# Two layers of a hybrid decoder on one core: the routing's combining weights made and spread behind the first two expert products

## The chip, the cores and the metric

The kernel runs on one core of a Trainium2 chip, as one program written by hand for five engines: TensorE (PE in the profile), VectorE (DVE), ScalarE (ACT), GpSimd (POOL) and SyncE (SP), which issues the large transfers. The metric is the device time of one execution in microseconds (us), lower is better.

## The reference

Two layers (`DEPTH = 2`) over 256 prompt tokens and 32 sample tokens, model width 1024, all in float32. Each layer mixes the tokens with three kinds of recurrent heads, projects back, normalises, and then sends each token through two of 32 experts. The expert part is what the change touches:

```python
def _moe(h, router_w, router_bias, p):
    scores = jax.nn.sigmoid((ht @ router_w).astype(jnp.float32))
    choice = (scores + router_bias.astype(jnp.float32)).reshape(T, N_EXPERT_GROUPS, EXPERTS_PER_GROUP)
    ...
    expert_idx = g_idx * EXPERTS_PER_GROUP + local
    wts = jnp.take_along_axis(scores, expert_idx, axis=1)
    wts = wts / jnp.sum(wts, -1, keepdims=True)
    ...
    def expert_block(args):
        xb, e = args
        return (jax.nn.silu(xb @ p["e_gate"][e]) * (xb @ p["e_up"][e])) @ p["e_down"][e]
    ...
    contrib = (ys[dest] * wts.reshape(A)[order][:, None]).astype(ht.dtype)
```

Of an expert, gate and up are 1024 x 512 and down is 512 x 1024: 2 MB each, 6 MB an expert, 32 experts a layer.

## The kernel before

There is no scheduler. Each engine's program is a function (`_(sp)`, `_(pe)`, `_(act)`, `_(dve)`, `_(pool)`), its instructions run in the order in which the code stands, and engines wait for each other by semaphores. `Signal.at(l, k)` is the k-th event of layer `l`; `stand(eng)` marks a wait in a way that has no part in the result. Of PSUM's eight banks six rotate through a list, `bank_plan()`: each entry names a result and who takes it away ("A" ScalarE, "D" VectorE). `emptied(l, key)` is the event that the bank which `key` will fill is free, `takes(l, key)` that `key` has been taken away, `fills(l, key)` that TensorE has filled it.

At the end of a layer's mixer the routing runs like this. TensorE turns the normalised rows (`turn_half`, `turn_few`, result `h2t`), multiplies them with the router (`logits`: 24 products for three tiles of tokens, tile 0 and 1 with 128 tokens, tile 2 with 32), turns the rows back (`turn_back`, `back`) and spreads the gate rows (`spread`). VectorE picks two experts a token from the scores (`oh_ready` when it is done). TensorE then counts with triangular products which place each token has in its expert's block (`rank`), and VectorE makes of it the 0/1 matrix `sel` (`select`), with which TensorE gathers the tokens of 4 experts into slots (`gather`, 32 slots an expert, `BLK`; a quad of experts is 128 slots). ScalarE copies the gathered rows in two halves into `xTb` (`take_gather`; events `g_half` and `g_taken`). Beside that, VectorE makes the two combining weights of each token (`dtm[:, 1]`), lays them on diagonals (`diagonal(1)`, event `wdiag_ready`), and TensorE spreads them over all partitions with a product with ones (`rows_of`, results `wrow` 0 and 1, which VectorE copies into `dbc`). The same is done for slot numbers (`diagonal(0)`, `ddiag_ready`, `drow_full`). From `dbc` VectorE builds `selw`, which spreads the experts' outputs back to the tokens (`weights`, `spread_out`). VectorE also scales the normalised rows (`x1_done`) and plans the blocks that overflow (`bew`, `bei`, `npi`, event `plan_ready`).

The experts then go in pairs `d`, member `b`, with two weight buffers, `ring` for `b` = 0 and `ring1` (printed `ring_122`) for `b` = 1, each with room for gate, up and down of one expert. `gate_up` waits for the weights (`gu_full`), multiplies, and signals `u_full`; ScalarE's `silu` and VectorE's `hidden` follow; `down` multiplies with the down weights (`dn_full`) and signals `d_full`. SP orders gate and up of the next expert for a buffer at `u_full`, its down at `d_full`. The down weights of expert 2 alone have a place of their own, `early`, and are ordered once, ahead of the loop. `keep_clock(n)` is filler on TensorE: n products of 512 columns whose result nobody reads. In the first quad of experts SP's order is:

```python
                sp.wait_ge(x1_done.sem, x1_done.at(l, 1))
                idle["sp"].stand(sp)
                sp.dma_start(early[:].rearrange("p (k n) -> p k n", n=D_MODEL),
                             A["exp_w_down"][l, 2].rearrange("(p k) n -> p k n", k=4)).then_inc(early_full.sem, 16)
                sp.wait_ge(u_full, 2 * (seen + 1) + 1)
                experts(0, 2)
                sp.wait_ge(u_full, 2 * (seen + 1) + 2)
                experts(1, 3)
                sp.wait_ge(d_full, 2 * (seen + 1) + 2)
                experts_down(1, 3)
```

## Time and profile before

| | before |
|---|---|
| median of 3 runs | 1876.62 us (1869.5 to 1877.93) |
| profiled execution, own time | 1879.24 us |
| its span | 1877.4 us |
| granted TensorE clock, mean | 0.9 of full |
| PE busy | 1545.1 us, 82% |
| DVE busy | 744.8 us, 40% |
| ACT busy | 346.8 us, 18% |
| DMA, mean over the span | 302 GB/s, 567.56 MB |

The profile is of one execution, on the hardware. Busy shares are means over stages that have different limits: TensorE's 82% doesn't say that it is the limit of any one of them. A float32 product appears as two instructions in the trace, so that the 24 router products are 48 rows' worth; the order of the built program, shown below, counts each once.

### The profile page before, as it was taken

To read this page: it belongs to the slowest core of one execution; us is meant where nothing else is said; L and a number is where in the kernel's file an instruction comes from. 1 tells how busy PE (TensorE), PEld (TensorE's weight loads), DVE (VectorE), ACT (ScalarE), POOL (GpSimd) and SP (SyncE) were. 2 spreads that over 40 slices of the span, in tenths; PEclk is the share of its full clock that TensorE was granted. 3 is DMA by queue.
4 is the path that set the end of the run, shared out by engine and by line. 5 is a ranking of instruction groups with operands and counts; after the bars stand their busy time and mean duration, and the time that the engine had idled before them with its cause. 6 is when DMAs were issued, how large, how long until landed. Compare 5 with 4: busy or idle time off the path is not lost.

```text
span 1877.4 us, 29665 instructions
## 1 busy us (share of the span) xinstructions
PE 1545.1 (82%) x11834; PEld 849.0 (45%) x11834; DVE 744.8 (40%) x1706; ACT 346.8 (18%) x787; POOL 116.8 (6%) x168
## 2 busy tenths in 40 slices
PE   5999999998867776677889999999976677666795
PEld 2764543545433333334366555354543334333442
DVE  0253565767312221222535266585732222122226
ACT  0235321203101111010223532120210111011001
POOL 4000002200200000000020000211000000000000
PEclk8899999988978888888989899998988889888877
DMA  9453447557999999999954543746789999999993
GB/s 321 152 191 139 124 127 209 167 198 293 380 405 427 428 428 428 428 429 428 401 210 164 200 124 101 224 127 227 285 347 427 428 428 428 428 427 428 429 426 129
DMA packets 94567, 567.56 MB, mean 302 GB/s; under 512 B 8245, under 2 KB 9021, under 8 KB 69138
## 3 DMA queue, kind: packets, MB, share of 16 engines
q1 hardware_dynamic: 82578, 532.05, 70.2%
q0 software_dynamic: 11904, 34.34, 6.5%
q8 instruction: 57, 0.93, 0.2%
q14 instruction: 28, 0.23, 0.0%
HBM read 550.55 MB, written 15.81 MB: 302 GB/s over the span
## 4 chain that ended last, share of the span: by engine, by line
PE 52%; DMA 38%; DVE 5%; issue 2%; SPq 1%; DVEq 1%; ACT 1%; ACTq 0%
DMA ring<-in_exp_w_up 35%; PE ps L1550 10%; PE ps L1017 9%; PE ps L992 9%; PE ps L1387 3%; PE ps L1239 3%; DMA ring<-in_w_ada 3%; PE ps L856 2%; PE ps L999 2%; PE ps L1208 1%; PE ps L1143 1%; PE ps L1184 1%; PE ps L1373 1%; PE ps L1567 1%; SPq L623 1%
## 5 line engine op out<-in xcount | busy, mean ns | idle before, releaser
L1550 PE MATMUL ps<-ring,xTb 128*32 128x256 f32 x4224 | 332.2, 484 | 232.8 <-DMA ring<-in_exp_w_up 220.6
L1550 PEld LDWEIGHTS ps<-ring,xTb 128*32 128x32 f32 x4224 | 164.7, 138 | 400.2 <-issue 357.8
L2745 DVE TENSOR_TENSOR hb<-sg,ps 128x128 f32<-128x128 f32 x66 | 25.0, 379 | 475.4 <-ACT sg L1932 475.4
L1017 PE MATMUL ps<-ring,hT 128*128 128x512 f32 x384 | 171.4, 599 | 0.0
L992 PE MATMUL ps<-hT,ring 128*128 128x288 f32 x640 | 165.0, 417 | 4.7 <-DVE hT L2089 2.5
L1523 PE MATMUL ps<-sel,h_tm 128*128 128x128 f32 (+1 forms) x912 | 162.9, 306 | 0.0
L1523 PEld LDWEIGHTS ps<-sel,h_tm 128*128 128x128 f32 x912 | 124.4, 188 | 52.8 <-issue 22.6
L992 PEld LDWEIGHTS ps<-hT,ring 128*128 128x128 f32 x640 | 122.7, 194 | 42.6 <-issue 8.4
L1932 ACT ACTIVATE sg<-ps 128x128 f32<-128x128 f32 x66 | 18.3, 277 | 605.1 <-PE ps L1550 605.1
L1567 PE MATMUL ps<-ring,hTb 128*32 128x256 f32 x2048 | 126.7, 389 | 2.5 <-DVEq L2748 2.5
L2753 DVE COPY ys<-ps 32x256 f32<-32x256 f32 x124 | 52.6, 424 | 161.1 <-PE ps L1567 159.9
L1017 PEld LDWEIGHTS ps<-ring,hT 128*128 128x128 f32 x384 | 71.1, 190 | 98.7 <-issue 98.2
L1675 ACT ACTIVATE ys<-ps 32x256 f32<-32x256 f32 x140 | 52.2, 373 | 217.9 <-PE ps L1567 216.6
L1582 PE MATMUL ps<-ys,selw 128*128 128x512 f32 x136 | 69.5, 639 | 20.6 <-DVEq L2754 20.5
L1567 PEld LDWEIGHTS ps<-ring,hTb 128*32 128x32 f32 x2048 | 60.8, 111 | 46.2 <-issue 3.7
L856 PE MATMUL ps<-ring,cT 128*32 128x512 f32 x384 | 54.5, 674 | 14.9 <-DMA ring<-in_w_ada 14.6
L1239 PE MATMUL ps<-ring,hT 128*128 128x512 f32 x128 | 62.3, 644 | 2.8 <-DVE h_tm L2310 2.8
L2771 DVE TENSOR_TENSOR acc<-acc,ps 128x512 f32<-128x512 f32 x68 | 46.8, 688 | 39.8 <-PE ps L1582 39.8
L2126 DVE SCALAR_TENSOR_TENSOR cv<-raw,vecT,cv 128x312 f32<-128x312 f32 x96 | 52.2, 543 | 7.2
L1582 PEld LDWEIGHTS ps<-ys,selw 128*128 128x128 f32 x136 | 22.4, 194 | 62.2 <-issue 38.1
L1239 PEld LDWEIGHTS ps<-ring,hT 128*128 128x128 f32 x128 | 25.9, 208 | 33.7 <-issue 30.2
L2292 DVE TENSOR_TENSOR h0s<-h0s,tbh 128x512 f32<-128x512 f32 x32 | 22.2, 692 | 42.8 <-PE ps L1184 40.1
(503 smaller groups left out, 1687.7 us busy)
## 6 DMA issues: line engine op xcount, KB each, us to landing
ring<-in_exp_w_gate SPq DMA_DIRECT2D x66, 2048.0 KB, 18.7
ring<-in_exp_w_up SPq DMA_DIRECT2D x66, 2048.0 KB, 23.2
ring<-in_exp_w_down SPq DMA_DIRECT2D x64, 2048.0 KB, 24.8
ring<-in_w_ada SPq DMA_DIRECT2D x24, 2048.0 KB, 10.2
ring<-in_w_in SPq DMA_DIRECT2D x22, 2048.0 KB, 9.1
ring<-in_w_out SPq DMA_DIRECT2D x8, 2048.0 KB, 9.1
h0s<-in_state_ssd POOLq DMA_DIRECT2D x16, 512.0 KB, 7.2
out_ssd_s<-h0s POOLq DMA_DIRECT2D x16, 512.0 KB, 5.3
```

Source lines behind the costliest of these rows:

```text
L856: mm(o[32 * g:32 * g + 32, :], cT[:, k, :], w[:, k, :], start=(r == 0), stop=False, skip_group_check=True)
L992: last = mm(o[:, 0:T], w[:, k, m * P:(m + 1) * P], hT[:, k, :], start=(k == 0), stop=(k == KT - 1))
L1017: last = mm(o[:, :], hT[:, k, T0[i]:T0[i] + P], w[:, k, :], start=(k == 0), stop=(k == KT - 1))
L1239: last = mm(o[:, :], hT[:, k, T0[i]:T0[i] + P], w[k // 4][:, k % 4, a * 512:(a + 1) * 512], start=(k == 0), stop=(k == KT - 1))
L1387: last = mm(o[:, :], y(k, i), w[k // 4][:, k % 4, a * 512:(a + 1) * 512], start=(k == 0), stop=(k == 7))
L1523: last = mm(o, h_tm[0:ROWS[i], i, k * P:(k + 1) * P], sel[0:ROWS[i], i, 0:n], start=(i == 0), stop=(i == NT - 1))
L1550: last = mm(ps[32 * j:32 * j + 32, b, 0:2 * P], xTb[:, k, m * BLK:(m + 1) * BLK], w[:, 0:2, k * D_EXPERT + j * P:k * D_EXPERT + (j + 1) * ...
L1567: last = mm(ps[32 * c:32 * c + 32, 2 + b, 0:2 * P], hTb[:, b, j * BLK:(j + 1) * BLK], w[:, j * D_MODEL + c * 256:j * D_MODEL + (c + 1) * 256],
L1582: last = mm(o[:, :], selw[:, T0[i]:T0[i] + P], ys[:, a * 512:(a + 1) * 512], start=True, stop=True)
L1675: cp = lambda o_, i_: f(o_, i_, ACT.Copy)
L2126: stt(c_, r_[:, j:j + CVW], tap(j), c_, ALU.mult, ALU.add)
L2753: cpy(ys[m * BLK:(m + 1) * BLK, c * 256:(c + 1) * 256], ps[32 * c:32 * c + 32, 2 + b, 0:2 * P])
```

## The change

It moves work about within the routing and the first quad, in both layers, and adds or drops almost nothing:

- Four of tile 0's eight router products go ahead of the second tile's transposes, behind `keep_clock`, which there goes from 3 to 1 products.
- On VectorE the combining weights and their diagonals move from ahead of the rank to behind the scaling of the rows. The copy of the counts (`nblk`) moves from behind that scaling to ahead of it, and the plan of overflowing blocks (`block_plan`) into the first quad.
- On TensorE the weights' rows are no longer spread ahead of the gather, in `wrow` banks, but behind the first two gate and up products, together with the slots' rows, in banks 3, 4 and 5. Bank 3 is also the second down product's, which gets a wait for `drow_taken`.
- The first gate and up product waits for the first half of the gathered rows, and in its middle for the second.
- The order of the first quad becomes: product 0, product 1, rows, down 0, down 1, gather of half the next quad, product 2, two of the gather, down 2, product 3, two of the gather, down 3. ScalarE and VectorE follow it.
- `early` is loaded in two halves; the first no longer waits for `x1_done`.

The diff, cut to its core (the `stand` marks and the old waits for the `wrow` banks are left out):

```diff
-    out += [(("rank",), "D"), (("wrow", 0), "D"), (("wrow", 1), "D")]
+    out += [(("rank",), "D")]
...
                 sp.wait_ge(filled.sem, fills(l, ("back", 1, 1)))
                 idle["sp"].stand(sp)
+                third = early[:].rearrange("p (k n) -> p k n", n=D_MODEL)
+                third_src = A["exp_w_down"][l, 2].rearrange("(p k) n -> p k n", k=4)
+                sp.dma_start(third[:, 0:2, :], third_src[:, 0:2, :]).then_inc(early_full.sem, 16)
                 sp.wait_ge(x1_done.sem, x1_done.at(l, 1))
                 idle["sp"].stand(sp)
-                sp.dma_start(early[:].rearrange("p (k n) -> p k n", n=D_MODEL),
-                             A["exp_w_down"][l, 2].rearrange("(p k) n -> p k n", k=4)).then_inc(early_full.sem, 16)
+                sp.dma_start(third[:, 2:4, :], third_src[:, 2:4, :]).then_inc(early_full.sem, 16)
...
                 turn_few()
-                keep_clock(3)
+                pe.wait_ge(*emptied(l, ("logit",)))
+                pe.wait_ge(*takes(l, ("h2t", 0, 0)))
+                logits(0, range(4))
+                keep_clock(1)
...
-                keep_clock(2)
-                pe.wait_ge(wdiag_ready.sem, wdiag_ready.at(l, 1))
-                rows_of(bank(("wrow", 0)), 2, 0)
-                rows_of(bank(("wrow", 0)), 2, 1).then_inc(FL, 1)
-                rows_of(bank(("wrow", 1)), 2, 2).then_inc(FL, 1)
-                keep_clock(2)
+                keep_clock(4)
...
-                pe.wait_ge(*takes(l, ("wrow", 1)))
+                pe.wait_ge(*takes(l, ("ms", 10)))
+                pe.wait_ge(*takes(l, ("rank",)))
...
                     for k in range(KT):
+                        if k == KT // 2 and second_half is not None:
+                            pe.wait_ge(g_taken, second_half)
...
+                def first_quad():
+                    d0, d1 = pe.snap(pairs + 0), pe.snap(pairs + 1)
+                    pe.wait_ge(g_half.sem, g_half.at(l, 1))
+                    gate_up(d0, 0, 0, steady + 1)
+                    gate_up(d0, 1, 1)
+                    pe.wait_ge(wdiag_ready.sem, wdiag_ready.at(l, 1))
+                    rows_of(ps[:, 3, :], 2, 0)
+                    rows_of(ps[:, 3, :], 2, 1)
+                    rows_of(ps[:, 5, 2 * TS:], 2, 2)
+                    pe.wait_ge(ddiag_ready.sem, ddiag_ready.at(l, 1))
+                    rows_of(ps[:, 4, :], 0, 0)
+                    rows_of(ps[:, 4, :], 0, 1)
+                    rows_of(ps[:, 5, :], 0, 2).then_inc(drow_full.sem, 1)
+                    down(d0, 0)
+                    pe.wait_ge(drow_taken.sem, drow_taken.at(l, 1))
+                    down(d0, 1)
+                    pe.wait_ge(sel_ready, steady + 2)
+                    gather(0, 4, QS).then_inc(gq_full.sem, 1)
+                    gate_up(d1, 0, 2)
+                    gather(4, 6, QS)
+                    down(d1, 0, True)
...
                 for k in range(2):
-                    tt(rt[:, 5 + k], rt[:, 3 + k], rt[:, 0], ALU.mult)
-                D()
-                for k in range(2):
-                    V.tensor_reduce(dtm[:, 1, :, k], rt[:, 5 + k], AX_X, ALU.add)
-                D()
...
-                diagonal(1)
-                D().then_inc(wdiag_ready.sem, 1)
...
                 select(QS, 0)
+                cpy(nblk[:, 0, :], bank(("rank",))[:, 96:128]).then_inc(TD, 1)
...
                 dve.sem_inc(x1_done.sem, 1)
...
+                diagonal(1)
+                D().then_inc(wdiag_ready.sem, 1)
```

Three places in the built program's order. The first is TensorE between the first transposes of the turned rows (`ps<-con,x_tm`) and the end of the router products (`ps<-rw,hT`); `ps<-con` alone is filler. Before:

```order
L1430 MATMUL ps<-con,x_tm 128x128 x8
L1438 MATMUL ps<-con,x_tm 128x32 x8
L914 MATMUL ps<-con 128x512 x3
L1430 MATMUL ps<-con,x_tm 128x128 x8
L1444 MATMUL ps<-rw,hT 128x32 x8
L1444 MATMUL ps<-rw,hT 32x32 x8
L1444 MATMUL ps<-rw,hT 128x32 x8
```

and of the changed kernel:

```order
L1432 MATMUL ps<-con,x_tm 128x128 x8
L1440 MATMUL ps<-con,x_tm 128x32 x8
L1446 MATMUL ps<-rw,hT 128x32 x4
L916 MATMUL ps<-con 128x512
L1432 MATMUL ps<-con,x_tm 128x128 x8
L1446 MATMUL ps<-rw,hT 128x32 x4
L1446 MATMUL ps<-rw,hT 32x32 x8
L1446 MATMUL ps<-rw,hT 128x32 x8
```

Four router products have moved ahead, and two filler products are gone.

The second is TensorE from the last rank product to the second down product: `ps<-diag,con` and `ps<-diag_s,con` are the rows of weights or slots, `ps<-sel,h_tm` the gather, `ps<-ring,xTb` gate and up, `ps<-ring,hTb` down. Before:

```order
L1496 MATMUL ps<-rt,con 128x32
L914 MATMUL ps<-con 128x512 x2
L1502 MATMUL ps<-diag,con 128x256 x2
L1504 MATMUL ps<-diag_s,con 128x64
L914 MATMUL ps<-con 128x512 x2
L1536 REGISTER_ALU
L1523 MATMUL ps<-sel,h_tm 128x128 x24
L1546 ISA
L1547 ISA
L1550 MATMUL ps<-ring,xTb 32x256 x32
L1502 MATMUL ps<-diag,con 128x256 x2
L1504 MATMUL ps<-diag_s,con 128x64
```

which goes on with 6 gather products, the first down product and the second gate and up product. Of the changed kernel, from the filler on:

```order
L916 MATMUL ps<-con 128x512 x4
L1532 REGISTER_ALU
L1519 MATMUL ps<-sel,h_tm 128x128 x24
L1544 ISA
L1545 ISA
L1551 MATMUL ps<-ring,xTb 32x256 x32
L1545 REGISTER_ALU
L1551 MATMUL ps<-ring_122,xTb 32x256 x32
L1507 MATMUL ps<-diag,con 128x256 x2
L1509 MATMUL ps<-diag_s,con 128x64
L1507 MATMUL ps<-diag,con 128x256 x2
L1509 MATMUL ps<-diag_s,con 128x64
```

Both sets of rows stand behind two gate and up products, and the filler is in one piece.

The third is VectorE from the choice of experts (`rt<-rt 128x32`) to the first reading of the ranks (`rt<-rt,ps`). Before:

```order
L2613 TENSOR_TENSOR rt<-rt 128x32
L2621 TENSOR_TENSOR rt<-rt 128x96 x2
L2624 TENSOR_REDUCE dtm<-rt 128x3 x2
L2626 TENSOR_TENSOR stat<-dtm 128x3
L2628 TENSOR_TENSOR rt<-rt,nblk 128x96 x2
L2630 RECIPROCAL stat<-stat 128x3
L2632 TENSOR_REDUCE stat<-rt 128x3 x2
L2634 TENSOR_TENSOR dtm<-dtm,stat 128x6
L2642 TENSOR_TENSOR diag<-con,dtm 128x128 x4
L2642 TENSOR_TENSOR diag_s<-con,dtm 32x32 x2
L2651 TENSOR_TENSOR rt<-rt,ps 128x64
```

and of the changed kernel:

```order
L2645 TENSOR_TENSOR rt<-rt 128x32
L2653 TENSOR_TENSOR rt<-rt,nblk 128x96 x2
L2656 TENSOR_REDUCE stat<-rt 128x3 x2
L2670 TENSOR_TENSOR rt<-rt,ps 128x64
L2671 TENSOR_TENSOR rt<-rt,ps 32x32
L2670 TENSOR_TENSOR rt<-rt,ps 128x64
```

The weights and their diagonals are gone from here; they now follow the four multiplications that scale the rows.

## Rows read from the trace of the kernel before

**Rows 1.** The page: GB/s in 40 equal slices of the span.

```profile
GB/s 321 152 191 139 124 127 209 167 198 293 380 405 427 428 428 428 428 429 428 401 210 164 200 124 101 224 127 227 285 347 427 428 428 428 428 427 428 429 426 129
```

**Rows 2.** The page: the chain that ended last, by engine and line.

```profile
DMA ring<-in_exp_w_up 35%; PE ps L1550 10%; PE ps L1017 9%; PE ps L992 9%; PE ps L1387 3%; PE ps L1239 3%; DMA ring<-in_w_ada 3%; PE ps L856 2%; PE ps L999 2%; PE ps L1208 1%; PE ps L1143 1%; PE ps L1184 1%; PE ps L1373 1%; PE ps L1567 1%; SPq L623 1%
```

**Rows 3.** Windows around the routing of layer 0.

```profile
core 0: us, PE busy (x) PEld busy (x) DVE busy (x) ACT busy (x) POOL busy (x), PEclk, DMA share, GB/s
437.50:440.50 3.00, 3.00 (x16) 2.77 (x16) 1.03 (x4) 1.26 (x4) 0.00 (x0) 0.50 1.03 437
445.00:454.00 9.00, 9.00 (x37) 5.16 (x37) 7.88 (x34) 1.17 (x2) 0.00 (x0) 1.00 1.00 427
455.00:458.00 3.00, 3.00 (x19) 2.40 (x18) 2.63 (x6) 0.60 (x1) 0.00 (x0) 1.00 0.04 16
458.50:463.50 5.00, 2.25 (x14) 1.63 (x12) 4.28 (x19) 1.88 (x2) 0.00 (x0) 0.78 0.84 347
464.50:473.00 8.50, 7.47 (x68) 3.69 (x68) 2.62 (x7) 0.28 (x1) 0.00 (x0) 0.58 0.01 3
474.00:500.00 26.00, 22.54 (x325) 13.73 (x325) 8.03 (x19) 3.01 (x10) 4.42 (x9) 1.00 0.99 419
```

**Rows 4.** Timeline of SP, layer 0: start and length in us.

```profile
457.20 0.33 SPq L649 DMA_DIRECT2D early<-in_exp_w_down  x1
472.21 0.33 SPq L623 DMA_DIRECT2D ring<-in_exp_w_gate  x1
...
481.05 0.33 SPq L623 DMA_DIRECT2D ring<-in_exp_w_gate  x1
...
490.13 0.34 SPq L623 DMA_DIRECT2D ring<-in_exp_w_gate  x1
```

**Rows 5.** Timeline of PE, layer 0; idle time before and its releaser in brackets.

```profile
433.57 4.76 PE L1444 MATMUL ps<-rw,hT 128*128 128x32 f32 x48
...
447.07 1.98 PE L914 MATMUL ps<-con 128*128 128x512 f32 x4
448.92 1.10 PE L1502 MATMUL ps<-diag,con 128*128 128x256 f32 x4
...
450.31 1.98 PE L914 MATMUL ps<-con 128*128 128x512 f32 x4
452.24 8.51 PE L1523 MATMUL ps<-sel,h_tm 128*128 128x128 f32 x48
465.53 6.61 PE L1550 MATMUL ps<-ring,xTb 128*32 128x256 f32 x64 [4.78 <-DVE dbc L2734]
472.07 1.13 PE L1502 MATMUL ps<-diag,con 128*128 128x256 f32 x4
473.13 0.43 PE L1504 MATMUL ps<-diag_s,con 32*128 32x64 f32 x2
473.49 2.18 PE L1523 MATMUL ps<-sel,h_tm 128*128 128x128 f32 x12
475.60 1.93 PE L1567 MATMUL ps<-ring,hTb 128*32 128x256 f32 x32
477.35 3.64 PE L1550 MATMUL ps<-ring,xTb 128*32 128x256 f32 x64
```

**Rows 6.** Timeline of PE, layer 1.

```profile
1353.06 8.41 PE L1523 MATMUL ps<-sel,h_tm 128*128 128x128 f32 x48
1366.08 5.20 PE L1550 MATMUL ps<-ring,xTb 128*32 128x256 f32 x64 [4.61 <-DVE dbc L2734]
```

**Rows 7.** Timeline of SP, layer 1.

```profile
1371.35 0.33 SPq L623 DMA_DIRECT2D ring<-in_exp_w_gate  x1
```

**Rows 8.** Timeline of DVE, layer 0: first look at the ranks, last step of `sel`.

```profile
448.72 0.22 DVE L2651 TENSOR_TENSOR rt<-rt,ps 128x64 f32<-128x64 f32 x1
...
451.60 0.56 DVE L2675 TENSOR_TENSOR sel<-selt 128x384 f32<-128x384 f32 x1
```

**Rows 9.** Timeline of ACT, layer 0: gate rows and second gathered half.

```profile
445.01 1.19 ACT L1916 ACTIVATE gate<-ps 32x512 f32<-32x512 f32 x2 [0.40 <-PE ps L881]
...
460.79 0.60 ACT L1675 ACTIVATE xTb<-ps 128x512 f32<-128x512 f32 x1 [3.62 <-PE ps L1523]
```

More of the change, by code:

```diff
@@ L1465, in _ @@
                     turn_half(1, a)
-                pe.wait_ge(*emptied(l, ("logit",)))
-                idle["pe"].stand(pe)
                 pe.wait_ge(*takes(l, ("h2t", 0, 1)))
                 idle["pe"].stand(pe)
-                logits(0, range(KT))
+                logits(0, range(4, KT))
                 pe.wait_ge(*takes(l, ("h2t", 2)))
@@ L1938, in take_down, with quad @@
                     last.then_inc(ysa, 1)
-                with act.Fori(0, QUADS) as Q:
+                def quad(Q, first):
                     d0 = act.snap(pairs + 2 * Q)
+                    if first:
+                        for b in range(2):
+                            silu(d0, b)
                     for m in range(QUAD):
                         d, b = d0 + m // 2, m % 2
-                        silu(d, b)
+                        if not first or m > 1:
+                            silu(d, b)
                         if m == QUAD - 1:
@@ L2685, in _ @@
                 dve.sem_inc(x1_done.sem, 1)
-                cpy(nblk[:, 0, :], bank(("rank",))[:, 96:128]).then_inc(TD, 1)
-                D()
+                for k in range(2):
+                    tt(rt[:, 5 + k], rt[:, 3 + k], rt[:, 0], ALU.mult)
+                D()
+                for k in range(2):
+                    V.tensor_reduce(dtm[:, 1, :, k], rt[:, 5 + k], AX_X, ALU.add)
+                D()
+                tt(n1, dtm[:, 1, :, 0], dtm[:, 1, :, 1], ALU.add)
+                D()
+                V.reciprocal(n2, n1)
+                D()
+                tt(dtm[:, 1], dtm[:, 1], over(n2, 2), ALU.mult)
+                D()
+                diagonal(1)
+                D().then_inc(wdiag_ready.sem, 1)
                 ts(npi[:], nblk[:, 0, :], float(BLK - 1), None, ALU.add)
@@ L2738, in _ @@
                 spreads = dve.snap(tb + l * QUADS)
-                dve.wait_ge(gq_full.sem, gq_full.at(l, 2))
-                idle["dve"].stand(dve)
                 def hidden(d, b):
@@ L2774, in add_up, with first_quad, quad @@
                         D().then_inc(acc_taken, 1)
-                def quad(Q, first):
+                def first_quad():
+                    d0, d1 = dve.snap(pairs + 0), dve.snap(pairs + 1)
+                    for b in range(2):
+                        hidden(d0, b)
+                    dve.wait_ge(drow_full.sem, drow_full.at(l, 1))
+                    idle["dve"].stand(dve)
+                    for v, at in ((2, 3), (0, 4)):
+                        for i in range(2):
+                            cpy(dbc[:, v:v + 2, T0[i]:T0[i] + P], ps[:, at, i * 2 * P:(i + 1) * 2 * P].rearrange(
+                                "p (v t) -> p v t", v=2))
+                    cpy(dbc[:, 0:2, T0[2]:T], one_rows(ps[:, 5, 0:2 * TS]))
+                    cpy(dbc[:, 2:4, T0[2]:T], one_rows(ps[:, 5, 2 * TS:4 * TS]))
+                    D().then_inc(drow_taken.sem, 1)
+                    dve.wait_ge(gq_full.sem, gq_full.at(l, 2))
+                    idle["dve"].stand(dve)
+                    select(QS, QS)
+                    for b in range(2):
+                        take_down(d0, b, b)
+                    block_plan()
+                    V.memset(acc[:], 0.0)
+                    V.memset(accs[:], 0.0)
+                    weights(QS)
+                    for b in range(2):
+                        hidden(d1, b)
+                        take_down(d1, b, 2 + b)
+                        if b == 0:
+                            dve.sem_inc(early_used.sem, 1)
+                    add_up(spreads)
+                def quad(Q):
                     d0 = dve.snap(pairs + 2 * Q)
@@ L2782, in quad @@
                         if m == 0:
[L2783 to L2792 removed]
                             weights(QS)
                         take_down(d, b, m)
[L2795 to L2796 removed]
                     add_up(spreads + Q)
[L2799 removed]
+                first_quad()
                 with dve.Fori(1, QUADS) as Q:
[L2801 removed]
+                    quad(Q)
                 tail = dve.value_load(npi[0:1, 0:1], min_val=2, max_val=TAILMAX)
```

98 lines of the change are left out of this document (39 added, 59 removed).

## The prediction, made before the changed kernel ran

> **What bounds the kernel now.** I read the page first. Its row of GB/s [rows 1] has two long stretches at 427 to 429 and, before each, a valley with slices down to 100 to 230. The flat stretches are the expert products, whose weights stream in; the valleys are the mixers. The chain that ended last [rows 2] gives 35% of the span to one transfer, `ring<-in_exp_w_up`, far ahead of any line of TensorE. So in the flat stretches the stream of weights is the clock of the kernel: an instruction that ends earlier there is worth nothing unless the stream then starts earlier or pauses less. The question for this change is therefore when the stream stands still near the routing, and whose signal restarts it.
>
> The windows answer it [rows 3]: in layer 0 the stream runs at 427 GB/s from 445 to 454, carries 16 GB/s from 455 to 458, runs again in 458.5 to 463.5 (one piece of 2 MB, `early`), and from 464.5 to 473 carries 3 GB/s. From 474 on it is full again at 419. So about 14 us of layer 0 pass with idle DMA engines, in two pauses. The issues on SP [rows 4] give their ends: `early` goes out at 457.20, and the next weights (expert 2) at 472.21, when the first gate and up product is done. Between that issue and 490.13 nothing is late, since each order falls while the one before still flows.
>
> What makes 472.21 is read on TensorE [rows 5]: the gather starts at 452.24 and runs 8.51 us; then TensorE stands idle 4.78 us, and the row names the releaser, VectorE's copy of the spread weights into `dbc` (the `wrow` banks, which VectorE empties only after its whole block plan); then the first product takes 6.61 us, although the same 64 instructions take 3.64 us at 477.35. The difference is the granted clock, 0.58 in the window 464.5 to 473 [rows 3], half speed for most of it, after the idle time. Layer 1 is the same picture [rows 6]: gather at 1353.06, 4.61 us idle, product 5.20 us, order at 1371.35 [rows 7].
>
> **The change, part by part, as the time of the order for expert 2.**
>
> 1. Upstream of the gather, logits. Four of the 24 logit products (8 of 48 instructions) move ahead of the second transposes, where filler stood, and two of three filler products go. The 48 take 4.76 us [rows 5], so 8 are 0.8 us. The remaining logits need the same transposes as before, so the last logit comes 0.8 us earlier, and what follows in order on TensorE (turning back, spreading, the rank products) with it. The ranks end, read as the start of the filler at 447.07, near 446.3.
>
> 2. Between ranks and gather. Before: filler 1.98, weight rows from 448.92, filler again from 450.31, gather at 452.24 [rows 5], 5.2 us. After: four filler products in one go, twice 1.98 = 3.96, so TensorE is free at 450.3. VectorE's side: from its first look at the ranks at 448.72 to the end of `sel` (451.60 + 0.56) it needs 3.4 us [rows 8], and it no longer makes the combining weights and their diagonals before that look, so it looks when the ranks are there, near 446.5, and is done near 450.0. The gather starts at 450.3: 1.9 us earlier (0.8 of it from point 1).
>
> 3. Gather to first product. The wait on `dbc` is gone: minus 4.78 and 4.61 us [rows 5, 6]. What is asked instead is the first half of the gathered rows, copied by ScalarE while the second half is still gathered, and, in the middle of the product, the second half. That second copy starts at 460.79 and takes 0.60 us [rows 9]; the gather ended at 460.75, so the half is there about 0.65 us after the gather, and TensorE asks for it after half a product, 1.8 us. No wait; if the product did have to wait for it whole, 0.65 us would come back. I take off 4.6 a layer, leaving 0.1 for the signals.
>
> 4. The first product at full clock. With no idle time ahead of it, it should take the 3.64 us of the row at 477.35: minus 3.0 in layer 0, minus 1.6 in layer 1 (5.20). The bound below is nothing, if the clock falls anyhow.
>
> Sum: 1.9 + 4.7 + 3.0 = 9.6 us in layer 0, 1.9 + 4.5 + 1.6 = 8.0 in layer 1, together 17.6 us. The order for expert 2 falls at about 462.6 instead of 472.21.
>
> 5. The early piece in two halves. Its first half no longer waits for the normalised rows and queues behind the weights that flow until some 454.5 [rows 3]; the second goes out when the rows are scaled, 2 us earlier than 457.20 (the selection is 1.9 us earlier, its four multiplications are unmoved). 2 MB at 427 is 4.9 us, so both are in by about 460, ahead of the new order at 462.6. They fill a pause and cost and bring nothing; had the piece been left whole, the result would be the same to a microsecond. If they collide it is for at most 1 us a layer.
>
> 6. What the moved work costs behind the first products. The weights' chain and diagonals (from `rt` to `diag`, some 3 us) now stand behind the scaling on VectorE, ahead of the slot diagonals, whose end stays near 462. TensorE does two products first (until 466), then both sets of rows, 1.13 + 0.43 each [rows 5], until 469, the down product 1.93, a wait of a few tenths for VectorE's six copies out of the bank which the second down product overwrites, and that one until 473. Then the gather of 24 instructions, 4.4, which also needs `sel` again (VectorE: 1.7 us after the copies, near 472.6), and the third product: it ends 19 us after the order, near 481. The order for expert 4 hangs on it. Is the stream still flowing then? Ahead of it are 8 MB ordered at 462.6 and 466.2 and 2 MB at 473 (after the second down product; the 8 MB last until 482). 10 MB at 427 take 24.6 us, so the stream would run dry near 488.5. The cover is 6 to 7 us. The block plan and the zeroing of `acc`, 4 us of VectorE, lie between the down products and the third product's `silu`, which they just fit.
>
> So from 464 on the stream should never pause, and it carries the same bytes: a stream that restarts 9.6 us earlier ends 9.6 us earlier, and everything behind it, the next layer too, moves by that. The profiled execution took 1879.24 us (span 1877.4), 2.6 above the median of the three runs, 1876.62, which themselves spread over 8.4. 1879.2 - 17.6 = 1861.6 by its own time; against the median 1859.0, which I forecast.
>
> **Rivals.**
>
> A. The clock falls earlier. Before, filler ran right up to the second transposes, and even so the clock stands at 0.50 in 437.5 to 440.5 [rows 3], at the end of the logits and in the turning back. After, the filler is a third, with a short wait ahead of it for the first turned rows. If the clock falls at the start of the remaining logits (40 instructions, 3.95 us), the ratio of the two product rows, 6.61 to 3.64, makes at most 3.2 us more; half of that is likelier. 1.5 to 3.2 a layer: 1862 to 1865.5. For it: the logits alone did not hold the clock in either layer. Against it: the full clock of the window 445 to 454, where filler and ranks stand, is reached either way, and the last filler is denser than before. The other way, if the clock did not fall at all, the turning back would gain, but VectorE's choice of experts then sets the ranks, 0.9 us at most a layer: 1857.
> The Trainium skill's page "TensorE: Matmul & The Clock Gate" (Part 1, on the clock gate) says that half clock is the array's default and that activity releases it; this speaks against taking filler out, and the half clock in the logits' window agrees with it. By that rule alone all remaining logits would run at 1.2 GHz, an estimate at the upper end of this rival.
>
> B. The stream runs dry again. If the third product ends more than 6 to 7 us later than near 481, because `sel`, the copies from the shared bank or the third product's rows hold TensorE, each further microsecond is lost one to one. Six extra microseconds beyond the cover in each layer leave 17.6 - 12 = 5.6: 1871. For it: many new waits stand in a row between the second and third product. Against it: each is under 2 us by its row.
>
> C. Slower. The clock falls in the logits and stays half through filler, gather and first product. At 6.61 to 3.64 the gather's 8.51 grows by 6.9, the product by 3.0, the filler by 3.2, the logits by 3.2: 16.3 us against a gain of 9.6 and 8.0 that counts the product at full clock: about 15 us slower, 1892. It decides from 8.8 us a layer on, which filler and gather at half clock nearly reach alone. Against it: filler at full clock in the row at 447.07, four of them now without a break.
>
> D. The change doesn't do what it says: the first product starts no earlier, since another condition ends last (the gate rows or the copied slot counts, both asked ahead of it). The gate rows are taken by 446.2 [rows 9], the counts are copied right behind `sel`, 8 us ahead of need, so this takes an error in the reading. Only the 1.9 us a layer of points 1 and 2 would be left: 1873.
>
> **Numbers.** Forecast as summed 0.70 (its own range 1854 to 1863, from the spread of single runs and the 0.9 above and below); A 0.15; B 0.08; C 0.03; D 0.04. To be told from no change a difference here should pass 0.5%, 9.4 us: below 1867.2 it is faster. The forecast and A are, and B where it costs under 4 us a layer, half its chance; D and the rest of B are within it. Faster 0.89, same 0.08, slower 0.03. The range of 8 in 10 takes in A's end and the 8 us spread of the runs before: 1852 to 1867.
>
> **What would show it.** In the profile after: no idle time with `dbc` as releaser ahead of the first product; gather near 450.3; the first product 3.6 to 3.7 us, directly behind; the order for expert 2 near 462.6 in layer 0 and near 1353.7 in layer 1 (1371.35 less both gains); one pause in the stream of about 4 us, and none until the layer's end. Wrong would be: a granted clock of 0.5 over the gather; an idle row at the product's middle; a window under 400 GB/s between 480 and 500; or all these right and the end not moved, which would mean that the stream isn't the clock of the later stage.

## The result and the profile after

The changed kernel takes 1857.03 us in the median of four runs (1850.87 to 1857.92), beside 1877.28 for the kernel before: ratio 0.9894, 95% interval 0.9875 to 0.9913. Two later sets of six runs of the same kernel gave 0.9890 (0.9865 to 0.9914) and 0.9894 (0.9868 to 0.9920). The forecast was 1859.0, in 1852 to 1867. The profiled execution took 1857.72, its span is 1855.9, 21.5 us under the span before, where the steps had said 17.6.

First the page, as in [rows 1, 2]: GB/s in 40 slices, and the head of the chain that ended last.

```profile
GB/s 325 165 182 141 127 128 211 164 196 338 416 412 427 428 428 429 428 428 428 355 231 137 231 125 85 203 151 207 299 370 427 428 429 428 428 428 429 428 427 188
...
DMA ring<-in_exp_w_up 38%; PE ps L1551 10%; PE ps L1019 9%; PE ps L994 9%; PE ps L1389 3%; PE ps L1241 3%; PE ps L1001 2%; PE ps L858 2%; DMA ring<-in_w_ada 1%; PE ps L1519 1%; PE ps L1210 1%; PE ps L1145 1%; PE ps L1186 1%; PE ps L916 1%; PE ps L1375 1%
```

The plateau still stands at 427 to 429: nothing became faster inside it. The two slices behind the first valley (the tenth and eleventh) rose from 293 and 380 to 338 and 416. Windows around layer 0's routing, to be held against [rows 3]:

```profile
445.00:454.00 9.00, 9.00 (x47) 6.24 (x46) 8.25 (x18) 0.60 (x1) 0.00 (x0) 1.00 1.01 421
...
456.00:460.00 4.00, 4.00 (x80) 2.45 (x76) 3.29 (x17) 1.18 (x2) 0.00 (x0) 1.00 0.37 88
...
464.00:500.00 36.00, 28.80 (x329) 16.49 (x331) 18.15 (x41) 4.63 (x12) 10.82 (x20) 0.98 1.01 425
```

One pause is left, inside 456 to 460, and from 464 to 500 the stream runs at 425 GB/s. The timeline of SP, as in [rows 4], gives what ends it:

```profile
438.51 0.33 SPq L649 DMA_DIRECT2D early<-in_exp_w_down  x1
451.49 0.33 SPq L652 DMA_DIRECT2D early<-in_exp_w_down  x1
458.62 0.33 SPq L623 DMA_DIRECT2D ring<-in_exp_w_gate  x1
...
462.07 0.33 SPq L623 DMA_DIRECT2D ring<-in_exp_w_gate  x1
...
469.09 0.33 SPq L628 DMA_DIRECT2D ring<-in_exp_w_down  x1
477.06 0.34 SPq L623 DMA_DIRECT2D ring<-in_exp_w_gate  x1
```

Expert 2 is ordered at 458.62, not 472.21. Of these 13.6 us, 3.8 are from an earlier stage (the first transposes start at 424.6, before at 428.4), and the rest, 9.8, is the routing. The timeline of TensorE shows the parts, as in [rows 5]:

```profile
442.82 3.70 PE L916 MATMUL ps<-con 128*128 128x512 f32 x8
446.46 8.51 PE L1519 MATMUL ps<-sel,h_tm 128*128 128x128 f32 x48
454.90 7.11 PE L1551 MATMUL ps<-ring,xTb 128*32 128x256 f32 x128
461.94 1.13 PE L1507 MATMUL ps<-diag,con 128*128 128x256 f32 x4
...
464.78 1.93 PE L1568 MATMUL ps<-ring,hTb 128*32 128x256 f32 x32
467.10 1.93 PE L1568 MATMUL ps<-ring,hTb 128*32 128x256 f32 x32 [0.39 <-DVEq L2814]
468.97 4.29 PE L1519 MATMUL ps<-sel,h_tm 128*128 128x128 f32 x24
473.19 3.66 PE L1551 MATMUL ps<-ring,xTb 128*32 128x256 f32 x64
```

No idle time stands ahead of the product, the first two run as one row of 128 instructions in 7.11 us, and there is no gap in its middle: ScalarE's second half starts at 455.01 and takes 0.60, as the row of ACT says.

```profile
455.01 0.60 ACT L1699 ACTIVATE xTb<-ps 128x512 f32<-128x512 f32 x1 [3.62 <-PE ps L1519]
```

In layer 1 the gain is smaller. TensorE from filler to product, as in [rows 6], with the router products ahead of it:

```profile
1324.55 2.05 PE L916 MATMUL ps<-con 128*128 128x512 f32 x2
1326.39 1.73 PE L1432 MATMUL ps<-con,x_tm 128*128 128x128 f32 x8
1327.96 3.61 PE L1446 MATMUL ps<-rw,hT 128*128 128x32 f32 x40
...
1344.57 8.51 PE L1519 MATMUL ps<-sel,h_tm 128*128 128x128 f32 x48 [0.29 <-DVEq L2695]
1353.01 7.11 PE L1551 MATMUL ps<-ring,xTb 128*32 128x256 f32 x128
```

The two filler instructions take 2.05 us, not the 1.1 of full clock (1.10 in layer 0), and the transposes 1.73 instead of 1.04: half clock for most of it, of which more below. SP's order, as in [rows 7], falls 35.5 us behind the first transposes, where layer 0 has 34.0.

```profile
1356.73 0.33 SPq L623 DMA_DIRECT2D ring<-in_exp_w_gate  x1
```

### The profile page after: what moved, and what is told of

It reads as the page before. It is cut to its first block, busy times and chain, and to the rows that moved or that the text cites. A ratio compares the mean times of both kernels' runs of the same rounds, so it can differ in the third digit from the quotient of the medians.

```text
span 1855.9 us, 29639 instructions
## 1 busy us (share of the span) xinstructions
PE 1536.3 (83%) x11826; PEld 844.1 (45%) x11826; DVE 744.7 (40%) x1706; ACT 331.8 (18%) x775; POOL 117.0 (6%) x168
## 4 chain that ended last, share of the span: by engine, by line
PE 53%; DMA 39%; DVE 3%; issue 2%; ACT 1%; SPq 1%; DVEq 1%; ACTq 0%
DMA ring<-in_exp_w_up 38%; PE ps L1551 10%; PE ps L1019 9%; PE ps L994 9%; PE ps L1389 3%; PE ps L1241 3%; PE ps L1001 2%; PE ps L858 2%; DMA ring<-in_w_ada 1%; PE ps L1519 1%; PE ps L1210 1%; PE ps L1145 1%; PE ps L1186 1%; PE ps L916 1%; PE ps L1375 1%
## 5 line engine op out<-in xcount | busy, mean ns | idle before, releaser
L1551 PE MATMUL ps<-ring,xTb 128*32 128x256 f32 x4224 | 325.8, 477 | 221.6 <-DMA ring<-in_exp_w_up 218.8
L1583 PE MATMUL ps<-ys,selw 128*128 128x512 f32 x136 | 69.5, 639 | 20.7 <-DVEq L2780 20.6
L1241 PEld LDWEIGHTS ps<-ring,hT 128*128 128x128 f32 x128 | 25.2, 202 | 32.7 <-issue 29.2
```

Of the source, the lines that this page charges most:

```text
L1241: last = mm(o[:, :], hT[:, k, T0[i]:T0[i] + P], w[k // 4][:, k % 4, a * 512:(a + 1) * 512], start=(k == 0), stop=(k == KT - 1))
L1551: last = mm(ps[32 * j:32 * j + 32, b, 0:2 * P], xTb[:, k, m * BLK:(m + 1) * BLK], w[:, 0:2, k * D_EXPERT + j * P:k * D_EXPERT + (j + 1) * ...
L1583: last = mm(o[:, :], selw[:, T0[i]:T0[i] + P], ys[:, a * 512:(a + 1) * 512], start=True, stop=True)
```

## The experiments

Twelve runs were made behind that of the changed kernel, two of them of the changed kernel itself, in three groups of four (e0_again, e3, e5, e1; then e4, e2, e6, e7; then e8, e10, e9 and e0_third), each group on one chip beside the kernel before. Single runs of one kernel spread over 3.5 to 16 us, so that the times alone part only large effects; each kernel's profile gives the stretches in which it differs. I cut every trace at the same seven marks: "to T" is the start up to the first transposes of layer 0; "R0" from there to the order for expert 2; "S0" to the last gate order of layer 0; "E0" to the first order of layer 1 (`in_w_ada`); "M1" to layer 1's first transposes; then R1, S1, E1 likewise, to the end of the span. In us, worked out as differences of start times in the timelines of SP and PE:

```
kernel               to T    R0     S0     E0     M1     R1     S1     E1    span
before               428.4  43.8  417.9   15.1  424.2   41.9  445.9   60.2  1877.4
changed              424.6  34.0  419.4   19.1  424.0   35.5  444.5   54.7  1855.9
e0_again             424.6  34.0  417.7   15.0  427.3   38.6  443.6   58.5  1859.3
e0_third             428.9  34.0  417.7   15.0  423.3   34.1  441.9   59.9  1854.8
e3_order_late        428.5  37.5  419.7   15.0  429.3   37.6  443.6   59.0  1870.2
e8_order_at_down     426.8  42.2  418.4   19.0  424.2   42.3  443.8   56.5  1873.2
e10_expert3_late     425.9  34.0  417.7   15.0  427.6   34.2  444.7   54.7  1853.8
e5_copy_first        426.8  38.5  418.6   15.0  429.0   38.3  445.3   58.2  1869.6
e1_no_halves         431.0  34.9  419.0   15.0  429.0   35.3  443.4   59.6  1867.3
e2_weights_first     427.5  35.5  416.3   15.0  427.8   35.0  443.5   59.6  1860.1
e4_early_alone       427.6  42.1  418.7   15.1  425.4   41.9  443.8   57.4  1872.0
e6_filler_three      425.1  34.2  417.3   15.1  424.1   34.2  441.9   57.2  1849.0
e7_half_orders       428.4  32.4  416.1   15.0  427.3   32.7  445.5   56.5  1854.0
e9_filler_halves     430.3  32.5  418.5   15.0  424.6   32.5  443.4   57.3  1854.1
```

R0 and R1 are what the change works on. The other six columns hold nearly the same work in every kernel (S0 and S1 begin with the reordered first quad), and still move by up to 6.4 us.

### The unchanged kernel twice more

No edit.

> The changed kernel once more, as the neighbour of the others and for a second trace. Theory (the order for expert 2 restarts the stream, and the end moves with it): from the first transposes of the turned rows to that order 34.0 us in layer 0 and 34 to 35.5 us in layer 1, as in the first trace (43.8 and 41.9 before); the end 16 to 20 us below the kernel before. In the first trace the stretch ahead of layer 0's transposes was 3.8 us shorter, the one between layer 0's order and layer 1's transposes 5.4 us longer, and the last one 6.9 us shorter than before. Rival (these belong to the change): the same signs and sizes here. Theory (they are the phase of the granted clock, by chance): other sizes, of either sign, in this trace.

> The changed kernel a third time, on the chip of the three others, as their neighbour. Theory: 0.988 to 0.991; layer 0's time from transposes to order 34.0 us again, layer 1's between 34.0 and 38.6 by the phase of the granted clock; the stretch before layer 0's transposes between 424 and 431 us, as in all traces so far. Rival (the stretch is 424.6 us in this kernel, as in its two traces so far, and longer in others): 424.6 us again.

Measured: 1856.32 us, ratio 0.9890 (0.9865 to 0.9914), and 1856.7 us, 0.9894 (0.9868 to 0.9920). R0 is 34.0 in all three traces. The odd stretches of the first trace (to T 3.8 shorter, S0 to M1 5.4 longer, E1 5.5 shorter) don't come back with the same sizes: to T is 424.6, 424.6 and 428.9, E0 19.1, 15.0, 15.0, E1 54.7, 58.5, 59.9. They aren't the change's. The rival of the third run, 424.6 each time, is wrong.

### The order for expert 2, late by a small and by a large dose

In e3 SP waits for the second product:

```diff
-                sp.wait_ge(u_full, 2 * (seen + 1) + 1)
+                sp.wait_ge(u_full, 2 * (seen + 1) + 2)
                 experts(0, 2)
```

> SP orders gate and up of expert 2 only when the second product is done, not the first; all else as changed. Theory: the order falls 3.4 to 3.6 us later in each layer, the pause of the stream is longer by as much, and the end comes 7 us later than the changed kernel, ratio to before about 0.993. Rival (the stream's restart isn't what sets the end, the gain came from the routing's shorter chain on TensorE): no change beyond 1 us, since no instruction of TensorE, VectorE or ScalarE stands elsewhere.

Measured: 1858.7 us, 0.9911 (0.9885 to 0.9937). In the trace the order is 3.5 us later in both layers (37.5 and 37.6, against 34.0 and 34.1). The time alone settles nothing: the median is 2.4 us above that of e0_again, its neighbour, where the theory had 7, and the interval takes in both. So the dose was made larger in e8:

```diff
-                sp.wait_ge(u_full, 2 * (seen + 1) + 1)
+                sp.wait_ge(d_full, 2 * (seen + 1) + 1)
                 experts(0, 2)
```

> The dose of the order's delay made larger: gate and up of expert 2 are ordered when the first down product is done (about 8 us behind the first product), all else as changed. Theory (the stream's restart sets the end): the order falls at 42 us from the transposes in both layers, near the 43.8 and 41.9 of the kernel before, the third product waits for its weights, and the end is 16 us later than the changed kernel, ratio 0.996 to 1.0, though every other part of the change is in. Rival (the gain is in the shorter work of the engines): ratio stays at 0.990 to 0.992.

Measured: 1875.9 us, ratio 1.0002 (0.9988 to 1.0016). The whole gain is gone, although every instruction of TensorE, VectorE and ScalarE stands where the change put it. SP's timeline, the windows and TensorE's third product in layer 0 of e8:

```profile
468.94 0.33 SPq L623 DMA_DIRECT2D ring<-in_exp_w_gate  x1
```

```profile
461.00:470.00 9.00, 8.61 (x120) 5.12 (x116) 4.04 (x14) 1.09 (x4) 0.00 (x0) 1.00 0.08 17
472.00:500.00 28.00, 21.19 (x236) 12.51 (x235) 8.21 (x20) 2.40 (x7) 6.24 (x13) 0.82 1.00 427
```

```profile
481.94 6.16 PE L1551 MATMUL ps<-ring,xTb 128*32 128x256 f32 x64 [6.52 <-DMA ring<-in_exp_w_up]
```

TensorE's first product ends where it does in the changed kernel (counted from the transposes), the stream stands still until the order (17 GB/s from 461 to 470), and TensorE then waits 6.52 us for the weights. The delay is 8.1 and 8.2 us, 16.3 in all; the timed difference to the neighbour e0_third is 0.0108 of 1876, 20 us, with an interval of some 5 us either way that takes 16.3 in. The rival, a gain in the engines' shorter work, is refuted. The third product itself takes 6.16 us behind this wait, 3.66 in the changed kernel: the granted clock from 472 to 500 is 0.82.

### The order for expert 3 late, that for expert 2 not

```diff
                 experts(0, 2)
-                sp.wait_ge(u_full, 2 * (seen + 1) + 2)
+                sp.wait_ge(d_full, 2 * (seen + 1) + 1)
                 experts(1, 3)
```

> The changed kernel, with the order for expert 3, not expert 2, held until the first down product is done, some 5 us later. Theory: the 4 MB of expert 2 still flow for 3 us then, so the stream has no pause and the end doesn't move (ratio 0.988 to 0.991); a delay counts only at the order that ends a pause. Rival (each order's delay counts, also of one behind a full stream): 10 us later, ratio 0.995.

Measured: 1854.29 us, 0.9880 (0.9853 to 0.9906). The order is 4.7 us later than in the changed kernel (8.2 us behind expert 2's instead of 3.5), and the stream doesn't notice. SP, and the windows:

```profile
459.90 0.33 SPq L623 DMA_DIRECT2D ring<-in_exp_w_gate  x1
...
468.06 0.33 SPq L623 DMA_DIRECT2D ring<-in_exp_w_gate  x1
```

```profile
465.00:470.00 5.00, 4.61 (x70) 2.70 (x68) 3.33 (x9) 0.75 (x2) 0.00 (x0) 1.00 1.01 424
470.00:475.00 5.00, 5.00 (x44) 3.61 (x40) 3.74 (x12) 0.75 (x2) 0.00 (x0) 1.00 1.02 433
```

So, of these two orders, lateness counts only at the one that ends the pause. The change also puts the second product ahead of the rows, and with it this order; e10 says that an order earlier by the rows' 3.1 us (1.13 and 0.43, twice) brings nothing by itself. The product's own place was not varied.

### The wait for the copied weights alone

On the kernel before, the copies of the weights' rows, behind that of the counts, move ahead of the scaling and the block plan:

```diff
                 select(QS, 0)
 
+                cpy(nblk[:, 0, :], bank(("rank",))[:, 96:128]).then_inc(TD, 1)
+                D()
+                dve.wait_ge(filled.sem, fills(l, ("wrow", 1)))
...
+                last.then_inc(TD, 1)
+                cpy(dbc[:, 2:4, T0[2]:T], one_rows(bank(("wrow", 1)))).then_inc(TD, 1)
+
                 for n_ in range(2):
                     for i in (1, 2):
```

> The kernel before with one edit: VectorE copies the spread weights out of their banks right behind the first selection, ahead of the scaling of the rows and the block plan; nothing else moves. It takes away the wait of the first product for that copy. Theory: the product starts when the second gathered half is copied, 0.7 us behind the gather (4.78 and 4.61 us before), at full clock or partly so, and the order for expert 2 falls 4 to 7 us earlier in each layer; the end 8 to 14 us earlier than before, ratio 0.993 to 0.996. Rival (the wait only hides the next one, for the second selection or the slot rows): the order is earlier, but the third product later by the same, and the end moves by less than 3 us.

Measured: 1866.71 us, 0.9941 (0.9920 to 0.9963). R0 is 38.5 and R1 38.3: 5.3 and 3.6 us off, half of the change's gain, by moved copies alone. TensorE in layer 0:

```profile
450.62 8.51 PE L1523 MATMUL ps<-sel,h_tm 128*128 128x128 f32 x48
460.00 5.15 PE L1550 MATMUL ps<-ring,xTb 128*32 128x256 f32 x64 [0.87 <-ACT xTb L1675]
```

The wait of 4.78 us shrank to 0.87, with ScalarE as the new releaser. The product takes 5.15, between full and half clock, in layer 1 5.35. The rival, that a later wait takes it back, is refuted by the end's 10 us.

### The halves of the gathered rows

```diff
-                    gate_up(d0, 0, 0, steady + 1)
+                    pe.wait_ge(g_taken, steady + 1)
+                    gate_up(d0, 0, 0)
```

> The changed kernel, but its first product waits for both gathered halves before it starts. Theory: TensorE idles 0.65 to 0.75 us ahead of the product, the order for expert 2 and the end come 0.7 us later a layer, 1.4 in all, which the end itself will hardly show. Rival (the short idle time lets the clock fall, as in the kernel before): the product takes 5 to 6.6 us instead of 3.6 in one or both layers, and the end comes 3 to 7 us later.

Measured: 1861.9 us, 0.9915 (0.9894 to 0.9936), not to be told from the changed kernel. R0 is 34.9, R1 35.3. The row of TensorE shows the idle time and the clock kept:

```profile
462.23 7.11 PE L1551 MATMUL ps<-ring,xTb 128*32 128x256 f32 x128 [0.87 <-ACT xTb L1700]
```

The halves are worth 0.9 us a layer (the idle time is 0.87 in layer 1 too), not through the clock: after the same 0.87 us, e5's product ran partly at half clock and this one at full. What decides is not in these two rows, and stays open.

### The weights' chain ahead of the ranks again

```diff
+                for k in range(2):
+                    tt(rt[:, 5 + k], rt[:, 3 + k], rt[:, 0], ALU.mult)
...
+                diagonal(1)
+                D().then_inc(wdiag_ready.sem, 1)
                 dve.wait_ge(filled.sem, fills(l, ("rank",)))
```

> The changed kernel, with VectorE making the combining weights and their diagonals ahead of the ranks again (as before), all else as changed: it isolates that move. Theory: VectorE comes to the ranks 3.6 us behind the choice instead of waiting 1.4 us for them, so 1.3 to 1.7 us later, the gather starts 1.2 to 1.7 us later, the order for expert 2 too: 35.3 to 35.7 us from the transposes in layer 0; the end 2.5 to 3.5 us later than the changed kernel. Rival (TensorE's filler sets the gather, VectorE has room): under 0.3 us a layer.

Measured: 1861.88 us, 0.9932 (0.9908 to 0.9955); the end alone can't tell 3 us from nothing here. R0 is 35.5, 1.5 us longer, and R1 35.0, 0.8 above the 34.1 of the third trace. TensorE waits for the selection:

```profile
445.69 3.70 PE L916 MATMUL ps<-con 128*128 128x512 f32 x8
450.81 8.51 PE L1519 MATMUL ps<-sel,h_tm 128*128 128x128 f32 x48 [1.42 <-DVEq L2709]
```

So moving the chain is worth 1.4 us in layer 0, and the filler doesn't hide it. In layer 1 the wait is 1.08 us, where the changed kernel has 0.29.

### The early piece alone, on the kernel before

The edit is the one of the change's diff on SP.

> The kernel before, with the early down weights in two halves, the first ordered without waiting for the scaled rows; nothing else. Theory: both halves fill a pause of the stream; transposes to order for expert 2 stay at 43.8 and 41.9 us, ratio 1.000 within the measurement. Rival (the earlier half makes the pause shorter and that counts): the end 2.4 us a layer earlier, 0.9975.

Measured: 1875.12 us, ratio 1.0004 (0.9984 to 1.0023). R1 is 41.9 as before; R0 is 42.1 instead of 43.8. The first product of layer 0 took 4.98 us in this trace, after the same 4.78 us of idle time, and 6.61 in the trace before: that is 1.6 of the 1.7 us, so this is the product's clock and not the piece. Splitting the piece brings nothing: the rival's 0.9975 is outside the interval.

### Filler back in front of the transposes

```diff
                 logits(0, range(4))
-                keep_clock(1)
+                keep_clock(3)
```

> The changed kernel with three filler products, not one, ahead of the second tile's transposes. In the second trace of the changed kernel layer 1's routing fell to half clock (13.7 us of it) with the logits at 6.30 us, and took 38.6 us against 34.0 in layer 0. Theory (the taken filler is what lets the clock fall there): with it back the full clock holds to the end of the logits in both layers, the transposes come 0.9 to 1.1 us later, 34.9 to 35.3 us to the order in both. Rival (the phase alone decides): layer 1 shows 37 us and more here too, or the time to the order is 36 and more with the filler's 2 us in full.

Measured: 1857.55 us, 0.9912 (0.9884 to 0.9940), no different in time. The traces show where the clock falls. TensorE in layer 1 of the second trace of the changed kernel (with one filler product), from the first router products on:

```profile
1320.92 1.81 PE L1446 MATMUL ps<-rw,hT 128*128 128x32 f32 x8 [0.69 <-ACT hT L1914]
1322.55 2.06 PE L916 MATMUL ps<-con 128*128 128x512 f32 x2
1324.40 1.92 PE L1432 MATMUL ps<-con,x_tm 128*128 128x128 f32 x8
1326.10 6.30 PE L1446 MATMUL ps<-rw,hT 128*128 128x32 f32 x40
1332.22 4.00 PE L1456 MATMUL ps<-con,hT 128*128 128x128 f32 x24
```

in layer 1 of the third trace of the same kernel:

```profile
1321.24 1.25 PE L1446 MATMUL ps<-rw,hT 128*128 128x32 f32 x8 [0.70 <-ACT hT L1914]
1322.31 2.05 PE L916 MATMUL ps<-con 128*128 128x512 f32 x2
1324.15 1.63 PE L1432 MATMUL ps<-con,x_tm 128*128 128x128 f32 x8
1325.62 3.50 PE L1446 MATMUL ps<-rw,hT 128*128 128x32 f32 x40
1328.95 2.82 PE L1456 MATMUL ps<-con,hT 128*128 128x128 f32 x24
```

and in layer 1 of e6, with three:

```profile
1318.13 1.05 PE L1446 MATMUL ps<-rw,hT 128*128 128x32 f32 x8 [0.71 <-ACT hT L1914]
1319.02 2.82 PE L916 MATMUL ps<-con 128*128 128x512 f32 x6
1321.68 1.04 PE L1432 MATMUL ps<-con,x_tm 128*128 128x128 f32 x8
1322.55 3.50 PE L1446 MATMUL ps<-rw,hT 128*128 128x32 f32 x40
1325.89 2.82 PE L1456 MATMUL ps<-con,hT 128*128 128x128 f32 x24
```

Two things are to be kept apart. The first is an early fall, in layer 1 alone: the filler runs at half clock (2.05 and 2.06 us for 1.10) in all three traces of the changed kernel, and the fall begins in the eight instructions ahead of the filler (1.15, 1.81 and 1.25 us in the three traces, for 1.05 at full clock). Up to there e6's TensorE has the same instructions, so the amount of filler behind can't be what started it. Of the nine traces with one filler product four show this fall in layer 1 (these three and e8's) and none in layer 0. e6 and e9, with three, don't show it; two traces, against five of nine without it, are no proof that filler prevents it. How long it lasts makes the price: R1 is 38.6 where the 40 router instructions fell too (6.30 us for 3.50), 35.5 in the first trace, and 34.1 in the third, where the clock came back in time for the turning back.

The second is the turning back (24 instructions). It takes 4.45 to 4.49 us in layer 0 of all nine traces with one filler product, 4.12 and 4.21 in the kernel before, and 2.82 in both layers of e6 and e9; the window from 1310 to 1350 of e6 shows a granted clock of 1.00. This is what three products behind the first router products do in every place seen. The two products more put the second transposes 1.7 us later; the router products behind them give 0.6 back (no wait for turned rows is left) and the turning back 1.6. The ranks then wait 0.38 us for VectorE, so nothing is gained either: R0 is 34.2 for 34.0, below the 34.9 to 35.3 that was expected.

### Half orders, alone and with the filler

```diff
-                sp.wait_ge(u_full, 2 * (seen + 1) + 1)
-                experts(0, 2)
+                sp.wait_ge(u_half.sem, u_half.at(l, 1))
+                idle["sp"].stand(sp)
+                for half, full in ((0, gu_first.sem), (1, gu_full[0])):
+                    if half:
+                        sp.wait_ge(u_full, 2 * (seen + 1) + 1)
+                    for j, name in enumerate(("exp_w_gate", "exp_w_up")):
+                        sp.dma_start(ring[:, j, :].rearrange("p (k n) -> p k n", n=D_EXPERT)[:, 4 * half:4 * half + 4, :],
+                                     A[name][l, 2].rearrange("(p k) n -> p k n", k=KT)[:, 4 * half:4 * half + 4, :]
+                                     ).then_inc(full, 16)
...
                     for k in range(KT):
                         if k == KT // 2 and second_half is not None:
+                            last.then_inc(u_half.sem, 1)
```

The third product waits for the first half's signal as well. In e9 `keep_clock(1)` ahead of the turning is `keep_clock(3)` too.

> The changed kernel, with the order for expert 2's gate and up in two halves: the first goes out in the middle of the first product, when half of the buffer has been read, the second at its end. Theory: the stream restarts 1.8 us earlier in each layer and the end comes 3 to 3.6 us earlier than the changed kernel, ratio near 0.987. Rival (the early half only waits for the second, or the two halves of four transfers cost as much as they bring): no change within 1 us.

> Three filler products again and the order for expert 2 in two halves, both at once on the changed kernel. Theory: 32.4 to 32.7 us from the transposes to the first half's order in both layers (34.0 to 38.6 in the changed kernel), the end 3 us earlier than with the filler alone, ratio 0.987 to 0.989. Rival (the halves' earlier start is lost in the stream behind, as their 1861.7 us alone would have it): the order as early, but the end at the changed kernel's or later.

SP in layer 0 of e7, the first and the second half of the gate:

```profile
460.80 0.33 SPq L660 DMA_DIRECT2D ring<-in_exp_w_gate  x1
...
462.45 0.33 SPq L660 DMA_DIRECT2D ring<-in_exp_w_gate  x1
```

The order falls 1.65 us earlier, as meant (R0 32.4, R1 32.7; in e9 32.5 in both). The end doesn't show it: 1861.67 us, 0.9925 (0.9898 to 0.9951), and 1857.32, 0.9894 (0.9871 to 0.9916) with the filler. e7's own forecast, 0.987, lies outside its interval; e9's, 0.987 to 0.989, lies partly inside. The 3.3 us looked for are less than the intervals' half width of 4 to 5 us, and the spans of 1854.0 and 1854.1 are no proof either, with a first stretch of 428.4 and 430.3. Whether any of the halves' gain reaches the end stays open, and what would take it back in e7 wasn't looked for; no version here is measurably better than the changed kernel.

## Why the prediction was right

**What bounds the kernel.** Right, and shown by e8 and e10 for the two orders that were delayed: the end follows the one that ends the pause of the stream, and not the next. It isn't a law to the microsecond: e7's order is 1.6 us earlier a layer and its end is not.

**Point 1 and 2, 1.9 us up to the gather.** From the first transposes to the gather there are 23.84 us before and 21.87 after in layer 0: 1.97. The total is right and its parts are not. The turning back starts 0.8 us earlier, as said (9.74 and 8.97 us behind the transposes), but takes 4.45 us for 4.12, so that the filler behind the ranks starts only 0.44 earlier (18.67 and 18.23), not 0.8; and from there to the gather are 5.17 and 3.64 us, 1.5 less and not 1.1. In layer 1, 23.63 and 23.37: 0.26 in the first trace. Here the term failed, in the way of rival A but earlier than A had it: the clock fell in the first router products, ahead of the filler, in all three traces, at a price of 1.4 us in the first, 4.5 in the second and nothing in the third (R1 35.5, 38.6, 34.1). A had it fall at the start of the remaining ones, in both layers, for 1.5 to 3.2 us; half of A came true, in one layer, with too low an upper end, because the filler, the transposes and the first router products run slowly too. Why it fell there, in layer 1 alone, stays open; the 0.7 us wait and the narrow products that now stand ahead of the filler are new at this place, and no run took them away again. The Trainium skill's page "TensorE: Matmul & The Clock Gate" (Part 1) says that activity releases the clock. The turning back agrees with it, at half clock behind one filler product (4.45 us) and at full clock behind three (2.82).

**Point 3, 4.7 and 4.5 us.** Gather to product: 13.29 before, 8.44 after in layer 0 (4.85), 13.02 and 8.44 in layer 1 (4.58). e5 shows that the moved copies alone would have had most of it (9.38 from gather to product in layer 0). e1 prices the halves at 0.9, where I had 0.65.

**Point 4, 3.0 and 1.6 us.** Product start to order: 6.68 and 3.72 in layer 0, 5.27 and 3.72 in layer 1, so 2.96 and 1.55. Right as to the product, which ran at full clock in every trace in which it followed the gather directly. The 3.0 of layer 0 depends on the one trace before: in e4, whose TensorE is unchanged, the product took 4.98 us and not 6.61, and against that the term is 1.3.

**Point 5.** Nothing; e4 agrees.

**Point 6, the cover.** The third product ended 18.2 us behind the order, predicted 19; no pause followed. The stream is not flat to the layer's end, though: from 506 to 512 it carried 344 GB/s with its engines busy (share 1.04), and the kernel before has the same from 520 to 526 (344, 1.03). Rivals B, C and D did not come. e10 spent 4.7 us of the cover of the order for expert 3; the 6 to 7 us of the order for expert 4 were not tested.

**The sum.** 9.6 + 8.0 = 17.6 was predicted. Against the one trace before, the three traces of the changed kernel give 9.8 + 6.4 = 16.2, 9.8 + 3.3 = 13.1 and 9.8 + 7.8 = 17.6, in the mean 15.6; against e4's trace each would be 1.7 less. The timed medians differ by 20.2 us, by the interval 16 to 23, and in the two later sets by 20.6 and 19.5. So the forecast fits the measured time, but the timed gain is some 4 us more than the two routings show in these traces, and where that lies stays open. The first span's 21.5 is 16.2 and luck: 3.8 us ahead of the routing, 5.5 in the last stretch, less 4.0 at layer 0's end.

## What to carry to other kernels

Where a stream of weights is the bound, find its pauses, name the signal that ends each, and count only what moves that signal: here 8 us of delay a layer on one order undid the whole change, and 4.7 us on the next order did nothing. Before reordering a stage, look at which copy a bank's release hangs on: copies moved ahead of a long chain brought half of this gain. Filler on TensorE is best judged by the granted clock of what stands ahead of it and behind it, over several traces: one kernel, at one place, lost 1.4, 4.5 and 0 us in three.

## What the runs showed of the hardware

The same instructions ahead of the routing took 424.6 to 431.0 us in fourteen traces. The granted clock goes with what I looked at: at the start of the first trace before it was 0.66 from 30 to 45 us, after 0.77, and the same 16 instructions took 3.56 and 1.92 us (timelines of TensorE, before and after):

```profile
34.39 3.56 PE L907 MATMUL ps<-con,qkvg 128*128 128x9 f32 x16 [0.44 <-issue]
```

```profile
34.76 1.92 PE L909 MATMUL ps<-con,qkvg 128*128 128x9 f32 x16 [0.45 <-issue]
```

At layer 0's end (E0) it was 19.1 us instead of 15.0 in the first trace after, with a clock of 0.73 in the window from 878 to 897 (1.00 before, from 890 to 905), while the stream ran at 428 and 427: between these two orders no row of TensorE waits for a weight. In the last stretch (E1) the clock was 0.75 before and 0.89 after, 60.2 and 54.7 us. So the stretches that differ between traces of one kernel are, as far as these windows show, those in which TensorE and not the stream sets the pace. That the clock is the whole cause, or that this is the spread of the single runs, wasn't tested.
